# An attention stage in which scores are issued three query tiles ahead and exponentials two, over three buffers of probabilities

## The chip, the cores and the metric

One NeuronCore of a Trainium2 chip runs the whole program. The metric is the device time of one execution, in microseconds (us). TensorE (PE) does matmuls and transposes, VectorE (DVE) maxima, divisions and subtractions, ScalarE (ACT) exponentials and copies, GpSimd (POOL) some copies and subtractions; SyncE (SP) issues the DMAs.

## The reference

One layer of a streaming encoder over 1024 tokens with 1024 features: a norm and an input projection, four retention heads, four attention heads, an output projection, a feed-forward part, a gated embedding and a last norm. The change touches only the attention heads:

```python
def attend(args):
    q_blk, b = args                                   # 128 queries
    q_chunk = (b * Q_BLOCK + jnp.arange(Q_BLOCK)) // CHUNK
    mask = key_chunk[None, :] <= q_chunk[:, None]     # causal by chunks of 64
    s = jnp.einsum('bqhd,bkhd->bhqk', q_blk, k).astype(jnp.float32) * scale
    s = jnp.where(mask[None, None], s, neg)
    prob = jax.nn.softmax(s, axis=-1).astype(v.dtype)
    return jnp.einsum('bhqk,bkhe->bqhe', prob, v)
```

Query tile t (0 to 7) sees the first (t+1)*128 keys, so tile 0 has 128 columns of scores and tile 7 has 1024. All is float32: a projection or a score is taken as hi*hi + hi*lo + lo*hi, with each operand split by ACT (the high part, a cast) and DVE (the rest, a subtraction).

## The kernel before, in words

Five engines run five instruction streams written out by hand, which meet at counting semaphores. Each stream is in order. The attention stage has four heads; heads 0 to 2 are iterations of a loop and head 3 stands by itself after it. One head is one pass of `pe_head` (line 1016), `act_head` (1077) and `dve_head` (1115), each with its own loop over the eight query tiles:

- `scores(t)` on PE (line 1032): five matmuls into one bank of PSUM for tiles 0 to 3, ten into two banks for tiles 4 to 7. `SCORE_BANK` (line 1009) names the first bank. From tile 4 on, banks are used again, and the matmuls wait for an earlier exponential (`a_exp`).
- `biggest(t)` on DVE (lines 1122 to 1127): masks the corner, takes the row maximum and scales it into a bias.
- `exp(t)` on ACT (line 1083): the exponential into a buffer of probabilities, t % 2 of two, and the row's sum; `divide(t)` on DVE (lines 1139 and 1142) divides by it in place.
- `turn(t)` on PE (line 1039): t+1 transposes of the probabilities into banks 4 and 5; ACT copies them out (line 1111), which raises `a_pt`.
- `values(t)` on PE (line 1048): 2(t+1) short matmuls, which wait for that copy. `out_hi(t)` on ACT (line 1088) and `out_lo(t)` on DVE (line 1133) split the result.

The order of PE in heads 0 to 2, before: scores 0, 1, 2; scores 3, turn 0; values 0, turn 1; scores 4, values 1, turn 2; scores 5, values 2, turn 3; scores 6, values 3, turn 4; scores 7, values 4, turn 5; next head's queries, first half, values 5, turn 6; second half of the queries, values 6, turn 7; both halves of the next head's keys, values 7. A half of the queries is six matmuls of 512 columns and a half of the keys three, all at line 860.

The order of ACT, before: exp 0; then for each t: exp t+1, out_hi t-1, the work of that step, and the copy of turn t. The work of a step is `early` at t = 3 (the casts of the next head's projection weights, lines 951 and 952), `out_weights_hi` at t = 4 and 5 (line 1070), and `late` at t = 7, which is the two casts of the next head's queries (line 983, `head_hi(e, h + 1, 0)`); `late` stands ahead of the copy of turn 7. After the loop come the casts of the keys and of the rotary rows, and out_hi 7.

The order of DVE, before: biggest 0, biggest 1, divide 0; then for each t: biggest t+2, divide t+1, out_lo t-1, and `early` at t = 3 (lines 956 and 958, the rest of the two weights).

In head 3 the two halves of the queries are replaced by transposes of the retention output (line 1235, four to a tile of 128 tokens): tiles 0 and 1 ahead of values 5, tiles 2 and 3 ahead of values 6; ACT and DVE take them out with `turned(0)` and `turned(1)`. After turn 7 comes the output projection (lines 206 to 208).

Of the kernel before, what the change touches and what calls it, by code (L numbers as in the profile page):

```python
# [17 lines left out]
ACT = mybir.ActivationFunctionType  # L18
AXX = mybir.AxisListType.X

P = 128
S = 1024
D = 1024
T = S // P
# [50 lines left out]
def build(nc, t_in, out):  # L75
    ctx = ExitStack()
    with ctx:
# [35 lines left out]
        def tmp(a, n):  # L113
            return TMP[:, a:a + n]
# [891 lines left out]

            return (1, (t + 1) * P) if t < 4 else (2, (t + 1) * P // 2)

        SCORE_BANK = (2, 0, 3, 1, 2, 0, 2, 0)

        def score_banks(t):

# [3 lines left out]
        def pe_head(e, h, early, after):  # L1016
            def scores(t):
                if t in (0, 3):
                    e.wait_ge(a_lo, h * 4 + (4 if t else 3))
                if t in (0, 2):  # L1020
                    e.wait_ge(a_qr, h * 2 + (2 if t else 1))
                if t >= 4:
                    e.wait_ge(a_exp, h * T + t - 1)
                tok = slice(t * P, t * P + P)
                nb, n = seen(t)
                for c in range(nb):

                    blk = slice(c * n, c * n + max(n, 2 * P))
                    dst = bank(SCORE_BANK[t] + c, max(n, 2 * P))
                    for i, (a, b) in enumerate(((QT[0], KT[0]), (QT[0], KT[1]), (QT[1], KT[0]),  # L1030
                                                (QR, CT[0][:, 3]), (QR, CT[1][:, 3]))):
                        last = nc.tensor.matmul(dst, a[:, tok], b[:, blk], start=(i == 0), stop=(i == 4))  # L1032
                last.then_inc(a_scores, 1)

            def turn(t):
                e.wait_ge(a_prob, h * T + t + 1)
                e.wait_ge(a_pt, h * T + t)
                for j in range(t + 1):
                    last = nc.tensor.transpose(PS[:, 4 + j // 4, (j % 4) * P:(j % 4) * P + P],  # L1039
                                               tmp((t % 2) * 1024 + j * P, P), ident)  # L1040
                last.then_inc(a_turn, 1)

            def values(t):
                e.wait_ge(a_vh, h * 2 + (1 if t < 2 else 2))
                e.wait_ge(a_pt, h * T + t + 1)
                e.wait_ge(a_o_lo, h * T + max(0, t - 1))
                for j in range(t + 1):
                    last = nc.tensor.matmul(bank(6 + t % 2, P), VH[:, j], PT[t % 2][:, j * P:j * P + P], start=(j == 0), stop=(j == t))  # L1048
                last.then_inc(a_pv, 1)

            for t in range(3):
                scores(t)
            for t in range(T):
                if t == 0:
                    scores(3)
                elif 2 <= t < T - 2:
                    scores(t + 2)
                elif t >= T - 2:

                    e.wait_ge(a_exp, h * T + T - 1)  # L1060
                    early(t + 2 - T)
                if t >= 1:
                    values(t - 1)
                turn(t)
            e.wait_ge(a_exp, h * T + T)
            after(lambda: values(T - 1))
# [10 lines left out]
        def act_head(e, h, early, late, after, turned=None):  # L1077
            def exp(t):
                e.wait_ge(a_bias, h * T + t + 1)
                e.wait_ge(a_turn, h * T + max(0, t - 1))  # L1080
                nb, n = seen(t)
                dst = tmp((t % 2) * 1024, nb * n).rearrange("p (b n) -> p b n", b=nb)
                nc.scalar.activation(dst, score_banks(t), ACT.Exp, bias=ST[:, 76 + t % 2:77 + t % 2],
                                     scale=SCALE, accum_out=ST[:, 78 + t % 2:79 + t % 2]).then_inc(a_exp, 1)

            def out_hi(t):
                e.wait_ge(a_pv, h * T + t + 1)
                nc.scalar.copy(HTH[:, bass.ds(h + 4, 1), t * P:t * P + P],
                               bank(6 + t % 2, P).unsqueeze(1)).then_inc(a_o_hi, 1)

            exp(0)
            for t in range(T):
                if t + 1 < T:
                    exp(t + 1)
                if turned and t == T - 1:
                    turned(1)
                if t >= 1:
                    out_hi(t - 1)
                if turned and t == T - 2:
                    turned(0)  # L1100
                if t == 3:
                    early()
                if t in (4, 5):
                    out_weights_hi(e, h, t - 4)
                if t == T - 1:
                    late()
                e.wait_ge(a_turn, h * T + t + 1)
                e.wait_ge(a_pv, h * T + max(0, t - 1))
                n = (t + 1) * P
                src = PS[:, 4:6, :].rearrange("p b n -> p (b n)")[:, 0:n]  # L1110
                nc.scalar.copy(PT[t % 2][:, 0:n], src).then_inc(a_pt, 1)
            after()
            out_hi(T - 1)

        def dve_head(e, h, early, after, turned=None):
            def biggest(t):
                e.wait_ge(a_scores, h * T + t + 1)
                e.wait_ge(a_exp, h * T + max(0, t - 1))
                src = score_banks(t)
                nb, n = seen(t)  # L1120

                nc.vector.memset(src[0:CHUNK, nb - 1, n - CHUNK:n], MASKED).then_inc(a_mask, 1)
                e.wait_ge(a_mask, h * T + t + 1)
                nc.vector.tensor_reduce(ST[:, 74 + t % 2:75 + t % 2], src, mybir.AxisListType.XY if nb > 1 else AXX,
                                        ALU.max).then_inc(a_max, 1)
                e.wait_ge(a_max, h * T + t + 1)
                nc.vector.tensor_scalar(ST[:, 76 + t % 2:77 + t % 2], ST[:, 74 + t % 2:75 + t % 2], -SCALE, None,
                                        ALU.mult).then_inc(a_bias, 1)

            def out_lo(t):  # L1130
                e.wait_ge(a_o_hi, h * T + t + 1)
                d = slice(t * P, t * P + P)
                nc.vector.tensor_tensor(HTL[:, bass.ds(h + 4, 1), d], bank(6 + t % 2, P).unsqueeze(1),
                                        HTH[:, bass.ds(h + 4, 1), d].bitcast(F32), ALU.subtract).then_inc(a_o_lo, 1)

            def divide(t):
                e.wait_ge(a_exp, h * T + t + 1)
                n = (t + 1) * P
                nc.vector.reciprocal(ST[:, 80 + t % 2:81 + t % 2], ST[:, 78 + t % 2:79 + t % 2]).then_inc(a_rec, 1)
                e.wait_ge(a_rec, h * T + t + 1)  # L1140
                p = tmp((t % 2) * 1024, n)
                nc.vector.tensor_scalar(p, p, ST[:, 80 + t % 2:81 + t % 2], None, ALU.mult).then_inc(a_prob, 1)

            biggest(0)
            biggest(1)
            divide(0)
            for t in range(T):
                if t + 2 < T:
                    biggest(t + 2)
                if t + 1 < T:  # L1150
                    divide(t + 1)
                if turned and t == T - 1:
                    turned(1)
                if t >= 1:
                    out_lo(t - 1)
                if turned and t == T - 2:
                    turned(0)
                if t == 3:
                    early()
            after()  # L1160
            out_lo(T - 1)

        def pe_3b(e):
            e.wait_ge(b_v_out, T)
            head_keys(e, 0, [0])
            rotary_turn(e, T - 1)
            e.wait_ge(b_qr, 5)
            head_keys(e, 0, [1])

            def next_keys(values, h):  # L1170
                head_keys(e, h)
                values()
            with e.Fori(0, HEADS - 1) as h:
                pe_head(e, h, lambda b: head_queries(e, h + 1, b), lambda values: next_keys(values, h + 1))
            e.wait_ge(r_done, NR)

            def first_turns(b):
                if b:
                    e.wait_ge(a_exp, NR)
                pe_retention_turn(e, (2 * b, 2 * b + 1))  # L1180

            def out_products(values):
                out_product(e, 0)
                values()
                pe_retention_turn(e, (4, 5))
                out_product(e, 1)
                pe_retention_turn(e, (6, 7))
            pe_head(e, HEADS - 1, first_turns, out_products)
# [1366 lines left out]
```

## Time and profile before

| | us |
|---|---|
| median of 3 runs | 1249.16 (1249.0 to 1249.78) |
| profiled execution, its own time | 1250.04 |
| profiled execution, span of the instructions | 1248.2 |
| PE busy by the page | 1235.0 (99%) |
| PE weight loads busy | 1042.3 (84%) |
| attention stage, from the first scores to the output projection | about 283 to 393 |

A row of the timeline gives the start, the length, the engine, the line, what is written and read, and how many instructions were merged; in square brackets stands the idle time before it and what ended it. A matmul's length includes its way through the array, so consecutive matmuls overlap in the rows, and the time that PE gives to one is read from the distance between starts. The windows view gives the busy time of each engine in a stretch.

### The profile page before, as it was taken

How to read it: one execution, taken by the hardware profiler on the slowest of the kernel's cores; microseconds unless marked ns; L12 is line 12 of the kernel's file. 1: busy time of each engine (PE TensorE's matmuls, PEld its weight loads, DVE VectorE, ACT ScalarE, POOL GpSimd, SP SyncE). 2: the span in 40 equal slices, each digit the busy share in tenths (PEclk: the TensorE clock that was granted, in tenths of full speed). 3: DMA queues.
4: the chain of work that ended last, by engine and by line, in shares of the span. 5: the costliest groups of instructions: out<-in, count | busy, mean ns of one | idle time of the engine just before them, and what ended most of it. 6: DMA issues, size and time to landing. Idle time of an engine off the chain costs nothing.

```text
span 1248.2 us, 16786 instructions
## 1 busy us (share of the span) xinstructions
PE 1235.0 (99%) x6014; PEld 1042.3 (84%) x6014; DVE 721.0 (58%) x1176; ACT 483.3 (39%) x892; POOL 516.2 (41%) x519
## 2 busy tenths in 40 slices
PE   9999999999999999999999999999999999999997
PEld 8888888888888888888888888888888888888886
DVE  5544444466664437855544455444489999954433
ACT  6622222256564224533333333333354344424422
POOL 3533443351110003555533455433499889810011
PEclk9999999999999999999999999999999999999999
DMA  9511101000021500242332342422554545420002
GB/s 342 166 34 42 44 2 43 1 10 26 17 92 62 152 1 1 76 127 93 118 114 70 113 127 85 127 85 85 185 192 160 171 169 187 150 85 1 1 34 101
DMA packets 101931, 115.09 MB, mean 92 GB/s; under 512 B 4832, under 2 KB 67680, under 8 KB 101856
## 3 DMA queue, kind: packets, MB, share of 16 engines
q1 hardware_dynamic: 101424, 113.57, 27.8%
q8 instruction: 45, 0.74, 0.2%
q10 hardware_dynamic: 432, 0.54, 0.1%
q14 instruction: 30, 0.25, 0.1%
HBM read 90.49 MB, written 23.59 MB: 91 GB/s over the span
## 4 chain that ended last, share of the span: by engine, by line
PE 95%; DVE 2%; ACT 1%; POOL 1%; issue 1%; DMA 0%; POOLq 0%; SPq 0%; DVEq 0%; ACTq 0%
PE PS L1738 11%; PE PS L1739 11%; PE PS L1737 11%; PE PS L208 8%; PE PS L206 8%; PE PS L207 8%; PE PS L2071 5%; PE PS L2073 5%; PE PS L2072 5%; PE PS L1032 3%; PE PS L1048 3%; PE PS L2450 2%; PE PS L2448 2%; PE PS L2449 2%; PE PS L2463 2%; PE PS L1039 1%
## 5 line engine op out<-in xcount | busy, mean ns | idle before, releaser
L206 PE MATMUL PS<-WF,HTH 128*128 128x512 f32 (+1 forms) x448 | 176.9, 395 | 0.5 <-DVE HTL L436 0.3
L208 PE MATMUL PS<-WF,HTL 128*128 128x512 f32 (+1 forms) x448 | 173.7, 388 | 0.0
L207 PE MATMUL PS<-WF,HTH 128*128 128x512 f32 (+1 forms) x448 | 173.3, 387 | 0.0
L1458 DVE TENSOR_TENSOR X<-X,PS 128x512 f32<-128x512 f32 x172 | 110.3, 679 | 53.4 <-PE PS L208 35.4
L1738 PE MATMUL PS<-HTL,WF 128*128 128x512 f32 x336 | 130.9, 389 | 0.0
L1737 PE MATMUL PS<-HTH,WF 128*128 128x512 f32 x336 | 130.9, 389 | 0.0
L1739 PE MATMUL PS<-HTH,WF 128*128 128x512 f32 x336 | 130.8, 389 | 0.0
L1670 DVE TENSOR_TENSOR WF<-RAW,WF 128x512 fp32r<-128x512 f32 x63 | 70.8, 1125 | 77.5 <-ACT WF L1660 77.5
L1739 PE MATMUL PS<-WF 128*128 128x512 f32 x252 | 98.1, 389 | 0.0
L1738 PE MATMUL PS<-WF 128*128 128x512 f32 x252 | 98.1, 389 | 0.0
L1737 PE MATMUL PS<-WF 128*128 128x512 f32 x252 | 98.1, 389 | 0.0
L206 PEld LDWEIGHTS PS<-WF,HTH 128*128 128x128 f32 x448 | 84.3, 188 | 16.4 <-DVE HTL L436 0.6
L208 PEld LDWEIGHTS PS<-WF,HTL 128*128 128x128 f32 x448 | 84.1, 188 | 16.3
L207 PEld LDWEIGHTS PS<-WF,HTH 128*128 128x128 f32 x448 | 84.3, 188 | 15.0
L1878 POOL TENSOR_TENSOR TMP<-TMP 128x512 f32<-128x512 f32 x10 | 16.1, 1608 | 160.3 <-DVE TMP L1862 160.3
L2072 PE MATMUL PS<-HTL,HTH 128*128 128x512 f32 x200 | 77.9, 389 | 0.0
L2071 PE MATMUL PS<-HTH 128*128 128x512 f32 x200 | 77.9, 389 | 0.0
L2073 PE MATMUL PS<-HTH,HTL 128*128 128x512 f32 x200 | 77.9, 389 | 0.0
L707 ACT ACTIVATE TMP<-PS,ST 128x384 f32<-128x384 f32 x32 | 18.6, 580 | 152.0 <-PE PS L208 152.0
L1737 PEld LDWEIGHTS PS<-HTH,WF 128*128 128x128 f32 x336 | 63.1, 188 | 13.1
L1738 PEld LDWEIGHTS PS<-HTL,WF 128*128 128x128 f32 x336 | 63.1, 188 | 13.1
L1739 PEld LDWEIGHTS PS<-HTH,WF 128*128 128x128 f32 x336 | 63.1, 188 | 13.0
(266 smaller groups left out, 2814.4 us busy)
## 6 DMA issues: line engine op xcount, KB each, us to landing
hid<-TMP SPq DMA_DIRECT2D x74, 256.0 KB, 2.3
TMP<-hid SPq DMA_DIRECT2D x25, 512.0 KB, 4.5
RAW<-in_w_ffn_gate SPq DMA_DIRECT2D x22, 512.0 KB, 4.0
RAW<-in_w_ffn_up SPq DMA_DIRECT2D x22, 512.0 KB, 5.3
RAW<-in_w_ffn_down SPq DMA_DIRECT2D x22, 512.0 KB, 4.1
X<-in_x SPq DMA_DIRECT2D x16, 512.0 KB, 6.6
RAW<-in_w_in SPq DMA_DIRECT2D x32, 256.0 KB, 3.8
TAB<-hid SPq DMA_DIRECT2D x9, 512.0 KB, 4.5
```

What stands on the lines that cost most here:

```text
L206: nc.tensor.matmul(dst, HTH[:, k, tok], w_h, start=(k == 0), stop=False)
L207: nc.tensor.matmul(dst, HTH[:, k, tok], w_l, start=False, stop=False)
L208: last = nc.tensor.matmul(dst, HTL[:, k, tok], w_h, start=False, stop=(k == K - 1))
L1032: last = nc.tensor.matmul(dst, a[:, tok], b[:, blk], start=(i == 0), stop=(i == 4))
L1458: nc.vector.tensor_tensor(x, x, src, ALU.add).then_inc(done, 1)
L1670: nc.vector.tensor_tensor(part(name, 1), part_raw(j, name), part(name, 0).bitcast(F32), ALU.subtract).then_inc(f_w_lo, 1)
L1737: nc.tensor.matmul(dst, w_h, m_h, start=(first and k == 0), stop=False, skip_group_check=True)
L1738: nc.tensor.matmul(dst, w_h, m_l, start=False, stop=False, skip_group_check=True)
L1739: last = nc.tensor.matmul(dst, w_l, m_h, start=False, stop=(k == 3), skip_group_check=True)
L2071: nc.tensor.matmul(dst, h_h, w_h, start=(q < 3 and k == 0), stop=False, skip_group_check=True)
L2072: nc.tensor.matmul(dst, h_h, w_l, start=False, stop=False, skip_group_check=True)
L2073: last = nc.tensor.matmul(dst, h_l, w_h, start=False, stop=(k == 1), skip_group_check=True)
```

## The change

- PE issues `scores(t + 3)` at step t, for t up to 4. Scores 4 move ahead of values 0, scores 5 ahead of values 1, and so on; each waits for the exponential that frees its banks (scores 4 for exp 1, scores 5 for exp 3, scores 6 for exp 4, scores 7 for exp 5).
- Tile 1 scores go to bank 3 and tile 2 scores to bank 0.
- The next head's queries go to steps 5 and 6, and the first half of its keys to step 7, ahead of values 6; the second half stays ahead of values 7. In head 3 retention tiles 0 and 1 go to step 5, tile 2 to step 6, tile 3 to step 7.
- ACT does exp 0 and exp 1 first and then exp t+2 at step t. `early` goes from step 3 to step 2 on ACT and on DVE. `late` stays at step 7.
- Probabilities, biases and sums have three buffers, t % 3; the third buffer of probabilities is the space `JUNK` (the tables of the angles, no longer in use). DVE's maximum and ACT's exponential wait one tile less.

```diff
-        SCORE_BANK = (2, 0, 3, 1, 2, 0, 2, 0)
+        SCORE_BANK = (2, 3, 0, 1, 2, 0, 2, 0)
+        BIAS, SUMS = 85, 88
+        def probs(t):
+            return JUNK if t % 3 == 2 else tmp((t % 3) * 1024, 1024)
 ...
                 if t >= 4:
-                    e.wait_ge(a_exp, h * T + t - 1)
+                    e.wait_ge(a_exp, h * T + (2 if t == 4 else t - 1))
 ...
             for t in range(T):
-                if t == 0:
-                    scores(3)
-                elif 2 <= t < T - 2:
-                    scores(t + 2)
-                elif t >= T - 2:
-                    e.wait_ge(a_exp, h * T + T - 1)
-                    early(t + 2 - T)
+                if t < T - 3:
+                    scores(t + 3)
+                else:
+                    e.wait_ge(a_exp, h * T + (T if t == T - 1 else T - 1))
+                    early(t + 3 - T)
                 if t >= 1:
                     values(t - 1)
                 turn(t)
 ...
             def exp(t):
                 e.wait_ge(a_bias, h * T + t + 1)
-                e.wait_ge(a_turn, h * T + max(0, t - 1))
+                e.wait_ge(a_turn, h * T + max(0, t - 2))
 ...
             exp(0)
+            exp(1)
             for t in range(T):
-                if t + 1 < T:
-                    exp(t + 1)
+                if t + 2 < T:
+                    exp(t + 2)
 ...
-                if t == 3:
+                if t == 2:
                     early()
 ...
             def biggest(t):
                 e.wait_ge(a_scores, h * T + t + 1)
-                e.wait_ge(a_exp, h * T + max(0, t - 1))
+                e.wait_ge(a_exp, h * T + max(0, t - 2))
 ...
+            def next_queries(b, h):
+                if b < 2:
+                    head_queries(e, h, b)
+                else:
+                    head_keys(e, h, [0])
             def next_keys(values, h):
-                head_keys(e, h)
+                head_keys(e, h, [1])
                 values()
 ...
             def first_turns(b):
                 if b:
                     e.wait_ge(a_exp, NR)
-                pe_retention_turn(e, (2 * b, 2 * b + 1))
+                pe_retention_turn(e, (b + 1,) if b else (0, 1))
```

## Rows read from the trace of the kernel before

**Rows 1.** The page: busy time of each engine, share of the span, instructions.
```profile
PE 1235.0 (99%) x6014; PEld 1042.3 (84%) x6014; DVE 721.0 (58%) x1176; ACT 483.3 (39%) x892; POOL 516.2 (41%) x519
```
**Rows 2.** Windows: head 1 and head 3; length, busy per engine, PEclk, DMA.
```profile
311.43:339.87 28.44, 27.76 (x190) 25.29 (x188) 18.40 (x55) 17.65 (x43) 3.54 (x3) 1.00 0.06 18
368.26:392.61 24.35, 23.68 (x171) 22.00 (x170) 16.67 (x51) 14.44 (x36) 3.61 (x3) 1.00 0.34 122
```
**Rows 3.** Timeline of the start of head 1: start, length, engine, line.
```profile
314.72 0.19 ACT L1083 ACTIVATION_READ_ACCUMULATOR TMP<-PS,ST 128x1 f32 x1
314.76 0.33 PE L1039 MATMUL PS<-CST,TMP 128*128 128x128 f32 x1
...
315.13 0.27 ACT L1111 COPY TMP<-PS 128x128 f32<-128x128 f32 x1 [0.22 <-PE PS L1039]
...
315.50 0.46 PE L1048 MATMUL PS<-TMP,GB 128*128 128x128 f32 x2 [0.40 <-issue]
...
316.12 0.44 PE L1039 MATMUL PS<-CST,TMP 128*128 128x128 f32 x2 [0.16 <-DVE TMP L1142]
...
316.36 0.71 PE L1032 MATMUL PS<-HTL 128*128 128x320 f32 x3
...
317.13 0.69 ACT L1083 ACTIVATE TMP<-PS,ST 128x512 f32<-128x512 f32 x1 [0.16 <-DVE ST L1127]
```
**Rows 4.** Timeline of head 1, steps 2 to 5.
```profile
317.94 0.61 PE L1048 MATMUL PS<-TMP,GB 128*128 128x128 f32 x4
...
318.33 0.82 DVE L1124 TENSOR_REDUCE ST<-PS 128x1 f32<-128x640 f32 x1
...
318.62 0.77 PE L1032 MATMUL PS<-HTL 128*128 128x384 f32 x3
...
319.37 0.80 ACT L1083 ACTIVATE TMP<-PS,ST 128x640 f32<-128x640 f32 x1
...
319.85 0.28 DVE L1133 TENSOR_TENSOR HTL<-PS,HTH 128x128 f32 x1
...
321.42 0.27 ACT L1088 CAST HTH<-PS 128x128 f32 x1 [1.16 <-PE PS L1048]
321.49 0.85 PE L1032 MATMUL PS<-HTL 128*128 128x448 f32 x3
321.62 0.41 ACT L951 CAST WF<-RAW 128x256 fp32r x1
...
322.14 0.58 ACT L1111 COPY TMP<-PS 128x512 f32<-128x512 f32 x1
...
322.78 0.41 DVE L956 TENSOR_TENSOR WF<-RAW,WF 128x256 fp32r<-128x256 f32 x1
...
324.96 0.93 PE L1032 MATMUL PS<-HTL 128*128 128x512 f32 x3
```
**Rows 5.** Timeline of the end of head 1.
```profile
332.51 1.63 PE L860 MATMUL PS<-WF 128*128 128x512 f32 x6
...
332.80 0.91 ACT L1111 COPY TMP<-PS 128x896 f32<-128x896 f32 x1 [0.41 <-PE PS L1039]
...
336.34 1.64 PE L860 MATMUL PS<-WF 128*128 128x512 f32 x6
...
336.95 1.05 ACT L1111 COPY TMP<-PS 128x1024 f32<-128x1024 f32 x1
...
338.09 2.02 PE L1048 MATMUL PS<-TMP,GB 128*128 128x128 f32 x16
```
**Rows 6.** Timeline of the end of head 3.
```profile
385.52 1.04 PE L1235 MATMUL PS<-CST,X 128*128 128x128 f32 x8
...
386.44 1.13 ACT L1083 ACTIVATE TMP<-PS,ST 128x1024 f32<-128x1024 f32 x1
...
386.66 1.58 PE L1048 MATMUL PS<-TMP,GB 128*128 128x128 f32 x12
...
390.04 1.80 PE L1048 MATMUL PS<-TMP,GB 128*128 128x128 f32 x14 [0.17 <-issue]
```

More of the change, by code:

```diff
@@ L1039, in turn @@
                     last = nc.tensor.transpose(PS[:, 4 + j // 4, (j % 4) * P:(j % 4) * P + P],
-                                               tmp((t % 2) * 1024 + j * P, P), ident)
+                                               probs(t)[:, j * P:j * P + P], ident)
                 last.then_inc(a_turn, 1)
@@ L1079, in exp @@
                 e.wait_ge(a_bias, h * T + t + 1)
-                e.wait_ge(a_turn, h * T + max(0, t - 1))
+                e.wait_ge(a_turn, h * T + max(0, t - 2))
                 nb, n = seen(t)
-                dst = tmp((t % 2) * 1024, nb * n).rearrange("p (b n) -> p b n", b=nb)
-                nc.scalar.activation(dst, score_banks(t), ACT.Exp, bias=ST[:, 76 + t % 2:77 + t % 2],
-                                     scale=SCALE, accum_out=ST[:, 78 + t % 2:79 + t % 2]).then_inc(a_exp, 1)
+                dst = probs(t)[:, 0:nb * n].rearrange("p (b n) -> p b n", b=nb)
+                nc.scalar.activation(dst, score_banks(t), ACT.Exp, bias=ST[:, BIAS + t % 3:BIAS + 1 + t % 3],
+                                     scale=SCALE, accum_out=ST[:, SUMS + t % 3:SUMS + 1 + t % 3]).then_inc(a_exp, 1)
             def out_hi(t):
@@ L1126, in biggest @@
                 e.wait_ge(a_max, h * T + t + 1)
-                nc.vector.tensor_scalar(ST[:, 76 + t % 2:77 + t % 2], ST[:, 74 + t % 2:75 + t % 2], -SCALE, None,
+                nc.vector.tensor_scalar(ST[:, BIAS + t % 3:BIAS + 1 + t % 3], ST[:, 74 + t % 2:75 + t % 2], -SCALE, None,
                                         ALU.mult).then_inc(a_bias, 1)
@@ L1138, in divide @@
                 n = (t + 1) * P
-                nc.vector.reciprocal(ST[:, 80 + t % 2:81 + t % 2], ST[:, 78 + t % 2:79 + t % 2]).then_inc(a_rec, 1)
+                nc.vector.reciprocal(ST[:, 80 + t % 2:81 + t % 2], ST[:, SUMS + t % 3:SUMS + 1 + t % 3]).then_inc(a_rec, 1)
                 e.wait_ge(a_rec, h * T + t + 1)
-                p = tmp((t % 2) * 1024, n)
+                p = probs(t)[:, 0:n]
                 nc.vector.tensor_scalar(p, p, ST[:, 80 + t % 2:81 + t % 2], None, ALU.mult).then_inc(a_prob, 1)
@@ L1157, in dve_head @@
                     turned(0)
-                if t == 3:
+                if t == 2:
                     early()
@@ L1168, in pe_3b @@
             head_keys(e, 0, [1])
+            def next_queries(b, h):
[3 more added lines that the diff above has]
+                    head_keys(e, h, [0])
             def next_keys(values, h):
-                head_keys(e, h)
+                head_keys(e, h, [1])
                 values()
             with e.Fori(0, HEADS - 1) as h:
-                pe_head(e, h, lambda b: head_queries(e, h + 1, b), lambda values: next_keys(values, h + 1))
+                pe_head(e, h, lambda b: next_queries(b, h + 1), lambda values: next_keys(values, h + 1))
             e.wait_ge(r_done, NR)
```

## The prediction, made before the changed kernel was built

> **What bounds the kernel now.** I read the page first: PE is busy for 1235.0 of 1248.2 us [rows 1], so whatever lengthens or shortens PE's stream changes the time one for one, and no change of order can win more than PE's idle time. The change adds and removes no matmul. Then the windows: head 1 takes 28.44 us from its first scores to those of head 2, with DVE busy for 18.40 and ACT for 17.65; head 3 takes 24.35 us up to the output projection [rows 2]. PE shows 27.76 of 28.44 us, an idle time of 0.68. That understates it, since the length of a matmul in a row includes its way through the array. I therefore took stalls from starts. A matmul of 512 columns takes 0.23 us of PE (0.09 more once per group), and a short one (values, transposes) about 0.10: seven of them lie between 317.94 and 318.62 [rows 4]. By starts head 1 waits in three places. The transpose of tile 0 starts at 314.76 and values 0 only at 315.50; two short matmuls later turn 1 starts at 316.12 [rows 3]. That is 0.62 and 0.33 us of waiting. And values 7 starts at 338.09, although six projections begun at 336.34 need 1.47 [rows 5]: 0.28 us.
>
> The Trainium skill (Trainium Kernel Development and Optimization, section Performance Expectations) says that matmul busy time is a bad measure because matmuls are pipelined, and that weight loads' busy time is a good one. Head 1 shows 25.29 us of them, 3.15 below the length [rows 2]. Taken as room that would be three times what I count by starts; most of it lies beside matmuls of 512 columns, so I keep the starts.
>
> All times below are us after the start of a head; head 1 starts at 311.43 [rows 2].
>
> **Part 1, the start of a head: what is removed comes back.** Scores 4 (1.58 us, 316.36 to 317.94) now stand between turn 0, at 3.33, and values 0. They wait for exp 1, whose last instruction ends at 314.91, 3.48 in [rows 3]: start 3.53, a wait of 0.1, end 5.11. ACT now does exp 2 ahead of copy 0 (old: 315.13), so that copy ends near 5.05 (an estimate: exp 2 lies half way between exp 1 and exp 3), just in time. Values 0 and turn 1 end at 5.55, and the old waits of 0.95 are gone. But scores 5 now stand next, and they wait for exp 3. Its row says what released it: a bias from DVE, at 5.70 [rows 3]. DVE's list up to there (three maxima, two divisions) is in the same order as before, so exp 3 does not come earlier. It ends at 6.39, its sum 0.09 later (as in the accumulator's row), and scores 5 start at 6.53: a wait of 0.98. In the old order scores 5 started at 318.62, 7.19 in, with values 1 and turn 2 (0.68) already done [rows 4]. The new one has these still ahead: 6.53 + 0.68 = 7.21. Nothing is gained. Bounds: -0.95 if DVE's bias came a microsecond earlier, which no row suggests, and 0; I take 0.
>
> **Part 2, scores 7 wait for exp 5: +0.85 in heads 0 to 2.** From exp 3 on, ACT and DVE release each other in a ring: exp t+2, out_hi t-1, out_lo t-1, the next maximum. After exp 3 (6.48) come out_hi 0 (0.27, of which 0.1 overlaps) and out_lo 0 (0.28 and about 0.15 to start): the maximum of tile 4 starts at 7.10. From the mask to the exponential it takes 0.15 + 1.04 (318.33 to 319.37), then exp 4 takes 0.80 + 0.09: end 9.19. The casts of the next head's weights, `early`, now come here, with out_hi 1 (0.20 to the next start) and 0.6 for both (321.62 to 322.14 and a tail) to 9.95; DVE's two subtractions (0.41 and a shorter one) last to 10.65 [rows 4]. Only then comes the maximum of tile 5, which stands behind them on DVE. With 0.13 us more for each further 128 columns in maximum and exponential, exp 5 runs from 12.0 to 13.0, and scores 7 can start at 13.05. PE is there earlier: scores 5 take 1.85 (321.49 - 318.62, less ten short matmuls), values 1 and turn 2 0.68, to 9.06; scores 6 wait for exp 4 until 9.24 and take 2.12 (324.96 - 321.49, less thirteen short ones); with values 2 and turn 3 that is 12.38. The wait is 0.7. The old scores 7 started at 13.53 with values 3 and turn 4 (1.35) done [rows 4]; the new state is 14.40, 0.87 later. Bounds: 0.1, if the ring takes 0.7 less, and 1.2, if each of its five hand-overs costs 0.07 more than read; I take 0.85.
>
> **Part 3, exp 7 goes ahead of copy 5: +0.2 in heads 0 to 2.** The maximum of tile 7 stands behind out_lo 3, which waits for values 3. By the same ring exp 7 ends near 20.2, 0.4 after ACT could have begun out_hi 4, and copy 5 is late by about 0.2 for values 5. Bounds 0 and 0.5.
>
> **Part 4, half as much work covers the copies at the end: +0.5 and +0.7 in heads 0 to 2.** The copy of tile 6 starts 0.29 after the six projections behind turn 6 and takes 0.91 (332.51, 332.80), so values 6 can start 1.30 after these [rows 5]. Six matmuls cover 1.47; now three keys matmuls stand there, 3 x 0.23 + 0.09 = 0.78: a wait of 0.52. Behind turn 7 ACT does the two casts of the queries before the copy, because `late` stays where it is, so values 7 start 1.75 after the projections (336.34 to 338.09) whatever PE does in between. They covered 1.47 and now cover 0.78: a wait of 0.97 in place of 0.28. The Trainium skill (TensorE: Matmul & The Clock Gate, Architectural detail) says that ACT and DVE are strict first-in, first-out queues. If ACT took the copy ahead of the casts, values 7 would wait some 0.5 less; the rows agree with the page, since the copy begins at 336.95, 0.6 after turn 7 had made way. Bounds of both waits together: 1.0 and 1.4. The moved queries save nothing: at their old places nothing waited.
>
> **Part 5, head 3: +1.8.** Nothing is cast at step 2, so scores 7 need not wait. At the end the cover is thinner. In the old order eight transposes (385.52 to 386.40) leave values 5 a wait of 0.26, a second eight leave values 6 0.33, and exp 7 runs at 386.44, after copy 5 [rows 6]. In the new one values 4 stand behind eight transposes (a wait of 0.3), values 5 behind four (0.45 us) and behind ACT's exp 7 (1.13), out_hi 4, a weight cast and copy 5 (a wait of 1.2 in all), values 6 behind four and one retention cast (0.8). That is 2.3 less 0.6: 1.7, with 0.1 of part 1's small waits. Bounds 0.6 and 2.6.
>
> **Sum.** Heads 0 to 2: 0.85 + 0.2 + 0.5 + 0.7 = 2.25 and 0.05 of small waits, 2.3 each, 6.9; head 3 1.8; together +8.7. The buffers cost no instruction, and SP's w_o loads wait for POOL as before, off the path. The profiled execution took 1250.04 and its span 1248.2, which would give a span of 1256.9; from the median of 1249.16 I predict 1257.9. The low ends give 3 x 1.1 + 0.6 = +3.9 (1253.1), the high ends 3 x 3.1 + 2.6 = +11.9 (1261.1).
>
> **Rivals.** A: the ring is faster than read and scores 7 do not wait, while the covers at the end still fall short: 8.7 - 3 x 1.05 = +5.5, 1254.7. For it: DVE has 10 of 28 us free. Against it: these are waits in a ring, not work. B: the waits at the head's start really go (-0.95 x 3 - 0.6 = -3.4), because the bias of tile 3 comes before PE is done with values 0, and only the ends cost (+3.6, and little in head 3): 1249.4. It decides at exp 3: it would have to end by 5.5 in place of 6.48. C, the other side: PE's run ahead absorbs everything, copies included, and all stalls go: 3 x 1.23 + 1.15 in head 3 = -4.8, less for head 0, so 1244.7. It decides at the copy of tile 7: it would have to be done 0.7 us earlier than the casts ahead of it allow. For it speaks only that a third buffer loosens two waits of ACT; no row shows ACT or DVE waiting for a buffer. D: DVE's or ACT's ring falls behind further than the bounds, each step costing PE up to 0.5 more: 1263. E: the change does nothing, because each stall only moves: 1249.2.
>
> **Chances.** The forecast 0.66, A 0.14, B and E together 0.10, C 0.07, D 0.03. The range runs from 1252.5 to 1261.5, with A inside and B to E (2 in 10) outside. About 0.2% (2.5 us) is what a measurement of this kernel can tell from no change: faster 0.07, same 0.10, slower 0.83.
>
> **What would show it.** Right: scores 5 start within 0.1 us of exp 3's accumulator read, 6.5 after the head's start; scores 7 start right behind exp 5; values 6 and values 7 start 1.3 and 1.75 after the keys' first matmul, the three matmuls of which end well before; a head of 30.7 us in place of 28.44 and PE's total busy time nearly unchanged. Wrong: scores 7 issued without a wait (A), or exp 3 earlier than 5.7 (B).

## The result: 10 us slower, and where the profile of the changed kernel shows it

| | before | changed |
|---|---|---|
| median, us | 1249.10 (6 runs, 1248.98 to 1249.78) | 1259.15 (6 runs, 1258.73 to 1259.38) |
| span of the profiled execution | 1248.2 | 1257.2 |
| its own time | 1250.04 | 1259.04 |

The ratio is 1.0079, with a 95% interval of 1.0069 to 1.0089. The forecast was 1257.9.

The page of the changed kernel, busy time of each engine (against rows 1), and the windows of head 1 and head 3 (against rows 2):

```profile
PE 1236.8 (98%) x6014; PEld 1040.1 (83%) x6014; DVE 721.0 (57%) x1176; ACT 482.5 (38%) x892; POOL 516.4 (41%) x519
```
```profile
313.30:344.28 30.98, 28.67 (x189) 25.09 (x188) 18.54 (x55) 17.38 (x43) 3.88 (x3) 1.00 0.06 17
375.24:401.61 26.37, 24.04 (x171) 21.99 (x170) 16.75 (x51) 14.37 (x36) 3.76 (x3) 1.00 0.32 112
```

Head 1 takes 30.98 us in place of 28.44, head 3 26.37 in place of 24.35 [rows 2]; heads 0 and 2 are longer by 2.54 and 2.57. Together the four heads take 9.67 us more. From the start of the output projection to the end both profiles take 855.59 us (1257.2 - 401.61 and 1248.2 - 392.61), so nothing is lost or won behind the stage. In front of it the changed kernel's profile is 0.67 us shorter (the first scores start at 282.59 and not 283.26), although no instruction there differs. That is a difference between executions, and with it the spans differ by 9.0.

The same engines do the same work in more time: DVE's and ACT's busy times hardly move. PE's own busy time even rises in head 1, from 27.76 to 28.67, though PE now waits more. A matmul's length includes its way through the array, and where the next one comes late, that way no longer lies under it. The weight loads keep their time in head 1 (25.29 us before, 25.09 now), so their share falls from 89% to 81%. The Trainium skill (Trainium Kernel Development and Optimization, Performance Expectations) says that weight loads' busy share and not matmul busy time tells how far a kernel is from full speed. These rows agree: matmul busy time rose while PE did the same work, and what the weight loads leave free of the head rose from 3.15 to 5.89 us, by 2.74 for a head that is 2.54 longer. Where PE waits is read from the starts.

The three largest waits of PE in the stage (who waited for whom, us in total, times, longest):

```profile
PE PS L1053 <- issue: 4.8, 8, 0.8
PE PS L1037 <- ACT TMP L1085: 2.8, 4, 0.7
PE PS L1037 <- ACT TAB L1085: 1.3, 3, 0.4
```

L1053 are the values, L1037 the scores, L1085 is the exponential. Scores now wait for exponentials; the same view of the kernel before has no such wait, only 1.8 us of values waiting and 0.3 of turns. "issue" ahead of values stands for ACT's copy: in the rows below the copy ends 0.1 us before each such start. The head's start, in the timeline of head 1 (start, length; the head begins at 313.30):

```profile
316.83 0.71 PE L1037 MATMUL PS<-HTL 128*128 128x320 f32 x3
...
318.07 0.26 ACT L1114 COPY TMP<-PS 128x128 f32<-128x128 f32 x1
...
318.43 0.46 PE L1053 MATMUL PS<-TMP,GB 128*128 128x128 f32 x2
318.72 0.38 PE L1044 MATMUL PS<-CST,TMP 128*128 128x128 f32 x2
...
318.99 0.69 ACT L1085 ACTIVATE TMP<-PS,ST 128x512 f32<-128x512 f32 x1 [0.67 <-DVE ST L1130]
...
319.58 0.19 ACT L1085 ACTIVATION_READ_ACCUMULATOR TMP<-PS,ST 128x1 f32 x1
...
319.82 0.79 PE L1037 MATMUL PS<-HTL 128*128 128x384 f32 x3 [0.72 <-ACT TMP L1085]
```

The reader is to see that the waits of rows 3 are gone (scores 4 at 316.83, values 0 and turn 1 right behind) and that one of the same size stands in their place. Turn 1 begins at 318.72 and takes 0.22, so PE is free at 318.94. Exp 3 begins 5.69 us into the head as before (5.70), its sum is read out by 319.77, and scores 5 start at 319.82, after 0.88 us of waiting. Steps 2 to 4:

```profile
321.58 0.79 ACT L1085 ACTIVATE TMP<-PS,ST 128x640 f32<-128x640 f32 x1 [1.39 <-DVE ST L1130]
...
322.59 0.41 ACT L951 CAST WF<-RAW 128x256 fp32r x1
...
323.35 0.42 DVE L956 TENSOR_TENSOR WF<-RAW,WF 128x256 fp32r<-128x256 f32 x1 [0.25 <-ACT WF L952]
...
323.98 0.11 DVE L1125 MEMSET PS<- 64x64 f32 x1
...
325.31 0.90 ACT L1085 ACTIVATE TAB<-PS,ST 128x768 f32<-128x768 f32 x1 [1.73 <-DVE ST L1130]
...
326.11 0.19 ACT L1085 ACTIVATION_READ_ACCUMULATOR TAB<-PS,ST 128x1 f32 x1
...
326.35 0.96 PE L1037 MATMUL PS<-HTL 128*128 128x512 f32 x3 [0.40 <-ACT TAB L1085]
```

This is the ring: casts on ACT, then their subtractions on DVE, only then the mask and maximum of tile 5 (from 323.98), exp 5, and scores 7 at 326.35. And the head's end:

```profile
337.03 0.94 PE L860 MATMUL PS<-WF 128*128 128x512 f32 x3
...
337.31 0.91 ACT L1114 COPY TMP<-PS 128x896 f32<-128x896 f32 x1 [0.41 <-PE PS L1044]
338.32 1.80 PE L1053 MATMUL PS<-TMP,GB 128*128 128x128 f32 x14 [0.34 <-issue]
...
340.75 0.94 PE L860 MATMUL PS<-WF 128*128 128x512 f32 x3
...
341.36 1.05 ACT L1114 COPY TMP<-PS 128x1024 f32<-128x1024 f32 x1
...
342.50 2.02 PE L1053 MATMUL PS<-TMP,GB 128*128 128x128 f32 x16 [0.81 <-issue]
```

Three keys matmuls begin at 337.03 and values 6 start 1.29 later; three begin at 340.75 and values 7 start 1.75 later, the same distance as from 336.34 to 338.09 before [rows 5], with half as much work in it.

### The profile page after: what moved, and what is told of

Same layout as the page of the kernel before. It is cut to its first block, busy times and chain, and to the rows that moved or that the text cites. A ratio compares the mean times of both kernels' runs of the same rounds, so it can differ in the third digit from the quotient of the medians.

```text
span 1257.2 us, 16787 instructions
## 1 busy us (share of the span) xinstructions
PE 1236.8 (98%) x6014; PEld 1040.1 (83%) x6014; DVE 721.0 (57%) x1176; ACT 482.5 (38%) x892; POOL 516.4 (41%) x519
## 4 chain that ended last, share of the span: by engine, by line
PE 92%; DVE 3%; issue 2%; ACT 2%; POOL 1%; DMA 0%; DVEq 0%; ACTq 0%; POOLq 0%; SPq 0%
PE PS L1747 11%; PE PS L1746 11%; PE PS L1748 11%; PE PS L206 8%; PE PS L208 8%; PE PS L207 8%; PE PS L2082 5%; PE PS L2080 5%; PE PS L2081 5%; PE PS L1053 2%; PE PS L2459 2%; PE PS L2458 2%; PE PS L2457 2%; PE PS L2472 2%; PE PS L1037 2%
```

## The experiments

Two questions were open: whether each term of the sum has the cause that the prediction gave it, and whether anything of the idea could be kept. In the labels a_ is an edit of the changed kernel and b_ one of the kernel before; the runs of before beside them had medians of 1249.18 to 1249.58.

**a_early3** undoes the move of the weights' casts.

```diff
-                if t == 2:
+                if t == 3:
                     early()
 ...
-                if t == 2:
+                if t == 3:
                     early()
```

The first place is ACT's, the second DVE's.

> The changed kernel (1259.15 us) with the casts of the next head's weights (early) back at step 3 on ACT and DVE. Theory (ring): the casts stand in the ring between exp 4 and the maximum of tile 5, so without them exp 5 ends about 1 us earlier and scores 7 no longer wait (0.56 us by starts in each of heads 0 to 2): -1.7, with up to 0.3 given back at exp 6: 1257.6. Rival (the wait for exp 5 has its cause in the order of exponentials and copies on ACT, not in the casts): unchanged, 1259.2.

Measured: 1257.93 us (ratio to before 1.0072, 1.0058 to 1.0086), 1.2 less than the changed kernel by the medians, though the slowest run (1258.94) reaches into the range of the changed kernel. In the profile each of heads 0 to 2 is 0.28 to 0.31 shorter and head 3 as long as in the changed kernel. The timeline of head 1:

```profile
323.93 0.91 ACT L1085 ACTIVATE TAB<-PS,ST 128x768 f32<-128x768 f32 x1 [1.32 <-DVE ST L1130]
...
325.19 0.94 PE L1037 MATMUL PS<-HTL 128*128 128x512 f32 x3
...
329.41 1.65 PE L860 MATMUL PS<-WF 128*128 128x512 f32 x6 [0.22 <-ACT TMP L1085]
```

Exp 5 begins 11.14 us into the head in place of 12.01, and scores 7 start without a wait, as the theory wanted, so the casts were what made scores 7 wait. Part of the gain comes back one step later: the casts now delay exp 6, and the queries wait for it, 0.38 us by starts. Moving the casts moves the wait and makes it smaller.

**a_keysback** puts the first half of the keys back behind turn 7.

```diff
                     head_queries(e, h, b)
-                else:
-                    head_keys(e, h, [0])
 ...
-                head_keys(e, h, [1])
+                head_keys(e, h)
                 values()
```

> The changed kernel with the first half of the next head's keys back behind turn 7, in heads 0 to 2. Theory (the cover is only divided anew): values 6 then wait 1.30 in place of 0.52 and values 7 0.28 in place of 0.98, together +0.1 per head: 1259.4. Rival (it is the early keys that cost, and values 6 would not wait without them): both waits go back to those of the kernel before, -1.2 per head, 1255.5.

Measured: 1259.46 us (1.0081, 1.0067 to 1.0095), no different from the changed kernel. In the timeline values 6 and values 7 of head 1:

```profile
339.00 1.80 PE L1053 MATMUL PS<-TMP,GB 128*128 128x128 f32 x14 [1.19 <-ACT TMP L1114]
...
343.18 2.02 PE L1053 MATMUL PS<-TMP,GB 128*128 128x128 f32 x16
```

Values 6 wait 1.35 and values 7 0.29, against 0.51 and 0.98 in the changed kernel: 1.64 in place of 1.49. The early keys are not what costs. What fits both divisions is that the run-ahead makes one more gap to cover. Before, all scores were issued by step 5 and eighteen projection matmuls covered three copies (5, 6 and 7). Now the scores are all issued by step 4 and the same eighteen must cover four.

**a_latefirst** puts ACT's casts of the next head's queries ahead of out_hi 6.

```diff
+                if t == T - 1:
+                    late()
                 if t >= 1:
                     out_hi(t - 1)
 ...
-                if t == T - 1:
-                    late()
                 e.wait_ge(a_turn, h * T + t + 1)
```

> The changed kernel with ACT's casts of the next head's queries (late) ahead of out_hi 6 in place of behind it. Theory (ACT's order): the copy of tile 7 then starts 0.3 after turn 7 and not 0.6, values 7 start 1.44 and not 1.75 after the keys' matmuls begin, and their wait falls from 0.98 to 0.66: -0.3 per head, 1258.2. Rival (the copy is held up by something else, as its own length or a buffer): 1259.2.

Measured: 1258.13 us (1.0071, 1.0057 to 1.0085), 1.0 less than the changed kernel, and its slowest run (1258.48) is below that kernel's fastest (1258.73). The rows of head 1:

```profile
340.24 0.94 PE L860 MATMUL PS<-WF 128*128 128x512 f32 x3
...
340.52 1.01 ACT L1114 COPY TMP<-PS 128x1024 f32<-128x1024 f32 x1 [0.52 <-PE PS L1044]
...
341.63 2.02 PE L1053 MATMUL PS<-TMP,GB 128*128 128x128 f32 x16 [0.46 <-issue]
```

The copy now begins 0.28 after the keys' first matmul and is released by PE's turn, where it began 0.61 after it, straight from the casts. Values 7 follow at 1.39 in place of 1.75, 0.36 earlier; the prediction had put this order at some 0.5. The statement quoted in the prediction from the Trainium skill (TensorE: Matmul & The Clock Gate, Architectural detail), that ACT takes its instructions strictly in order, is borne out: changing that order alone moved the copy.

**a_narrowmax** shortens DVE's list in front of exp 3; it leaves out part of the maxima.

```diff
+                if t < 4:
+                    src = src[:, :, 0:P]
                 nc.vector.tensor_reduce(ST[:, 74 + t % 2:75 + t % 2], src, mybir.AxisListType.XY if nb > 1 else AXX,
 ...
```

The lines left out put the factor 0.05 on the scale of tiles 0 to 3, in the exponential and in the bias.

> The changed kernel with the row maxima of tiles 1 to 3 taken over the first 128 columns alone (and a softmax scale a twentieth of the right one for tiles 0 to 3, so that nothing overflows): it leaves out part of the maximum. By the lengths of the reductions exp 3 comes 0.13 + 0.27 + 0.40 = 0.8 us earlier. Theory (scores 5 wait for exp 3, which DVE's list sets): the wait of 0.88 falls to 0.1 in all four heads and everything behind moves with it: -3.1, 1256.0. Rival (PE would be held there by a copy or the bank all the same): 1259.2.

Measured: 1255.94 us (1.0053, 1.0039 to 1.0067), 3.2 less. In head 1:

```profile
317.49 0.69 ACT L1085 ACTIVATE TMP<-PS,ST 128x512 f32<-128x512 f32 x1 [0.26 <-DVE ST L1132]
...
318.32 0.79 PE L1037 MATMUL PS<-HTL 128*128 128x384 f32 x3 [0.16 <-ACT TMP L1085]
```

Exp 3 is still released by DVE, and scores 5 again start 0.14 after its end, but the wait fell from 0.88 to 0.32 in heads 1 and 2 and is gone in heads 0 and 3 (head 0 waits 0.21 before scores 6 instead). In head 1 scores 5 start 0.80 earlier in the head than in the changed kernel (5.72 and not 6.52). The wait shrank by 0.56 of that; the rest is that PE reaches the place sooner, since scores 4 too wait for an exponential whose maximum is now shorter. The waits before scores 7 and at the head's end stayed as they were.

**b_narrowmax** does the same to the kernel before.

> The kernel before with the same narrow maxima of tiles 1 to 3 (and the same twentieth of the softmax scale for tiles 0 to 3); it leaves out part of the maximum. Theory (in the old order the start of a head waits first for copy 0, which DVE's maxima of tiles 1 to 3 do not set, and for 0.33 us for the division of tile 1): only that second wait goes, in heads 1 and 2, and 0.07 in the others: -0.8, 1248.3. Rival (DVE's list sets the start of a head whatever PE's order): -3, 1246.

Measured: 1248.30 us (0.9992, 0.9983 to 1.0001), 0.9 less by the medians, though the interval includes no change. The wait of 0.62 before values 0 is still there in each head (0.56 here) and the wait of 0.33 before turn 1 is gone. So the same shortening is worth 3.2 us in the changed order and less than 1 in the old one: only in the changed order is PE held by DVE's list at that place.

**b_actahead** keeps of the change ACT's and DVE's part alone; PE's order is that of before (a diff against the changed kernel). The lines left out put back the banks, the wait of scores 4, both halves of the keys behind turn 7 and the retention tiles two and two.

```diff
 ...
-                if t < T - 3:
-                    scores(t + 3)
-                else:
-                    e.wait_ge(a_exp, h * T + (T if t == T - 1 else T - 1))
-                    early(t + 3 - T)
+                if t == 0:
+                    scores(3)
+                elif 2 <= t < T - 2:
+                    scores(t + 2)
+                elif t >= T - 2:
+                    e.wait_ge(a_exp, h * T + T - 1)
+                    early(t + 2 - T)
 ...
```

> The changed kernel with PE's order of before (scores two ahead, queries at steps 6 and 7, both key halves behind turn 7, retention tiles two and two, banks of before), so only the exponentials two ahead, the three buffers and the early weights are left of the change. Theory (an exponential two ahead stands in front of the copy that values wait for, and needs its scores a step earlier to be free): each copy waits for the maximum and the exponential of the scores just made, 0.8 us more before values 0 and about 1, 0.4, 0.7 and 1.6 before values 2 to 5: +4.5 per head, 1267. Rival (ACT's order is free as long as it has idle time, and the cost of the change is PE's order alone): 1249.

Measured: 1261.78 us (1.0100, 1.0084 to 1.0115). The start of head 1, ACT and PE:

```profile
318.05 0.58 ACT L1088 ACTIVATE TAB<-PS,ST 128x384 f32<-128x384 f32 x1 [0.72 <-DVE ST L1133]
...
318.62 0.26 ACT L1117 COPY TMP<-PS 128x128 f32<-128x128 f32 x1
```
```profile
317.17 0.33 PE L1044 MATMUL PS<-CST,TMP 128*128 128x128 f32 x1
318.97 0.46 PE L1053 MATMUL PS<-TMP,GB 128*128 128x128 f32 x2 [1.47 <-issue]
```

Copy 0 stands behind exp 2, which waits for DVE, and values 0 wait 1.69 us, 1.07 more than before; that was expected. By starts the waits before values 2 to 5 are 0.92, 0.15, 0.2 and 1.07, where 1, 0.4, 0.7 and 1.6 were expected. The mechanism holds: the copy that values 2 wait for, at 323.82, stands behind exp 4, which waited 1.65 for DVE, and behind the casts of `early` (0.5 us). The total came out at +12.6 and not +18, because the sizes of the later waits were too high. A likely reason, not tested, is that each wait delays PE and so leaves the next copy more time.

**a_actold** is the other half: PE's scores three ahead, ACT's exponentials one ahead as before.

```diff
             exp(0)
-            exp(1)
             for t in range(T):
-                if t + 2 < T:
-                    exp(t + 2)
+                if t + 1 < T:
+                    exp(t + 1)
```

> The changed kernel with ACT's exponentials one tile ahead as before (exp t+1 at step t), all else as changed, so PE's scores run three ahead alone. Theory (the waits form a ring through banks: scores t+3 wait for exp t+1, which now stands behind the copy of tile t-1, which waits for PE's turn t-1): every step from scores 6 on waits for a whole round trip, by the same reckoning 1.7 us before scores 6, 1.9 before scores 7, 2.5 before the next head's queries: about +8 per head against 1249, 1280. Rival (the exponentials' lead is what costs, PE's alone is free): 1249 to 1253.

Measured: 1289.51 us (1.0326, 1.0311 to 1.0342). By starts head 1 waits 1.35 before scores 5, 1.98 before scores 6, 1.73 before scores 7 and 2.30 before the queries, and the head's end keeps its 0.51 and 0.98. The expectation had named 1.7, 1.9 and 2.5 and left out the first and the last two, and it had not foreseen a fall of PE's clock (last section). Each half of the change alone is worse than both together (1261.78 and 1289.51 against 1259.15). The banks bind the two leads to each other: from scores 5 on, scores t+3 need exp t+1 out of their way. No run has the third buffer by itself, so what it does alone is not shown.

**a_turns22** divides head 3's retention tiles two and two.

```diff
-                if b:
+                if b == 1:
                     e.wait_ge(a_exp, NR)
-                pe_retention_turn(e, (b + 1,) if b else (0, 1))
+                if b < 2:
+                    pe_retention_turn(e, (2 * b, 2 * b + 1))
```

> The changed kernel with head 3's retention tiles two ahead of values 4, two ahead of values 5 and none ahead of values 6 (two, one, one in the changed kernel). Theory (the cover is only divided anew): values 5 wait 0.4 less and values 6 0.4 more: 1259.2. Rival (the division of the retention tiles is what makes head 3 2.0 us longer): 1258.2 or less.

Measured: 1259.40 us (1.0076, 1.0062 to 1.0090), no different from the changed kernel. In head 3 values 5 and values 6:

```profile
396.15 1.57 PE L1053 MATMUL PS<-TMP,GB 128*128 128x128 f32 x12 [0.27 <-issue]
...
399.69 1.80 PE L1053 MATMUL PS<-TMP,GB 128*128 128x128 f32 x14 [1.20 <-ACT TMP L1114]
```

By starts values 5 wait 0.47 in place of 0.86 and values 6 1.35 in place of 0.77. The wait went from the one to the other, as with the keys: the same cover divided anew.

**b_split** asks what the lead in scores can be used for. It starts from the kernel before and moves half of scores 4 up, one bank of two; ACT and DVE keep their order.

```diff
-        SCORE_BANK = (2, 0, 3, 1, 2, 0, 2, 0)
+        SCORE_BANK = (2, 3, 0, 1, 2, 0, 2, 0)
 ...
-            def scores(t):
+            def scores(t, halves=None):
 ...
-                    e.wait_ge(a_exp, h * T + t - 1)
+                    e.wait_ge(a_exp, h * T + (2 if t == 4 else t - 1))
 ...
-                for c in range(nb):
+                for c in halves or range(nb):
 ...
-                last.then_inc(a_scores, 1)
+                if halves != (0,):
+                    last.then_inc(a_scores, 1)
 ...
                     scores(3)
-                elif 2 <= t < T - 2:
+                elif t in (1, 2):
+                    scores(4, (t - 1,))
+                elif 3 <= t < T - 2:
                     scores(t + 2)
```

> The kernel before (1249.1 us) with half of scores 4 (the bank of tile 0) moved ahead of values 0 and the other half left ahead of values 1; tiles 1 and 2 change banks as in the changed kernel; ACT's and DVE's order is that of before. Theory (exp 3 is the floor of a head's start, at 6.5 us, and the old order reaches scores 5 only at 7.19): half of scores 4 (0.75) fills the wait before values 0 and the other half the wait for copy 1, and scores 5 start at 6.53 with everything else done: -0.66 per head, less in heads 0 and 3 (0.5): 1246.8. Rival (moving scores up only moves the wait, as in the changed kernel): 1249.1.

Measured: 1246.65 us (0.9979, 0.9970 to 0.9988), 2.5 less than before. Head 1 begins at 310.13:

```profile
313.66 0.71 PE L1032 MATMUL PS<-HTL 128*128 128x320 f32 x3
...
314.50 0.38 PE L1049 MATMUL PS<-TMP,GB 128*128 128x128 f32 x2
...
314.81 0.44 PE L1040 MATMUL PS<-CST,TMP 128*128 128x128 f32 x2
...
315.00 0.68 PE L1032 MATMUL PS<-HTL 128*128 128x320 f32 x3
...
315.82 0.62 PE L1049 MATMUL PS<-TMP,GB 128*128 128x128 f32 x4
...
316.67 0.77 PE L1032 MATMUL PS<-HTL 128*128 128x384 f32 x3
```

Every group follows the one before it: half of scores 4, values 0, turn 1, the other half, values 1, turn 2, scores 5 at 6.54 in the head in place of 7.19. They start 0.08 after the sum of exp 3 is read out (316.59), so PE meets this floor with a wait of 0.1 at most. Both waits at the head's start are filled and nothing is taken from the head's end; in the profile the four heads are 0.66, 0.68, 0.62 and 0.61 shorter than in the kernel before.

**b_split_ends** adds the order of ACT at the end, as an edit of b_split.

```diff
+                if t == T - 1:
+                    late()
                 if t >= 1:
                     out_hi(t - 1)
-                if turned and t == T - 2:
-                    turned(0)
 ...
-                if t in (4, 5):
-                    out_weights_hi(e, h, t - 4)
-                if t == T - 1:
-                    late()
 ...
                 nc.scalar.copy(PT[t % 2][:, 0:n], src).then_inc(a_pt, 1)
+                if turned and t == T - 2:
+                    turned(0)
+                if t in (4, 5):
+                    out_weights_hi(e, h, t - 4)
```

> As b_split, and on ACT three copies of turned probabilities go ahead of casts that nobody waits for: the query casts stand ahead of out_hi 6 (as in a_latefirst), the output weights' casts behind copies 4 and 5, and in head 3 the cast of retention tile 0 behind copy 6. Theory (values wait for copies that stand behind casts): values 7 lose their wait of 0.28 in heads 0 to 2, and head 3 its waits of 0.26 and 0.33: -1.4 against b_split, 1245.4. Rival (these casts come back as waits of DVE, POOL or exponentials): equal to b_split.

Measured: 1245.65 us (0.9972, 0.9961 to 0.9983), the fastest of all and 3.5 under the kernel before. The step from b_split is 1.0, less than their intervals are wide, but the two sets of times do not overlap (1245.46 to 1246.26, and 1246.46 to 1246.84). The wait of values 7 is gone in heads 0 to 2, which is 0.85 by starts. Head 3 kept its two waits (0.23 and 0.33), against the expectation:

```profile
381.53 1.04 PE L1238 MATMUL PS<-CST,X 128*128 128x128 f32 x8
...
381.73 0.80 ACT L1110 COPY TMP<-PS 128x768 f32<-128x768 f32 x1 [0.39 <-PE PS L1040]
...
382.63 1.58 PE L1049 MATMUL PS<-TMP,GB 128*128 128x128 f32 x12
```

ACT is idle for 0.39 before this copy and is released by PE's turn, so no cast held it. The copy's own way from turn to values (1.1 us) is longer than eight transposes.

## Why the prediction was right

The measured 1259.15 lies between 1252.5 and 1261.5, and the mechanism came out as told in every part that a run took apart; only small terms were mis-sized. The predicted figure stands in brackets behind the measured one.

- **Part 1** held to 0.01 us in head 1: exp 3 at 5.69 (5.70), scores 5 at 6.52 (6.53), no gain at the start. a_narrowmax and b_narrowmax show the cause. PE reached the place at 5.64 (5.55), so the wait was 0.88 (0.98).
- **Part 2**: scores 6 at 9.22 (9.24), exp 5 from 12.01 to 13.00 (12.0 to 13.0), scores 7 at 13.05 (13.05). a_early3 shows that without the casts at this step scores 7 do not wait. PE was ready later than reckoned and waited 0.56 (0.7), with the four transposes ahead of it counted at the 0.11 us that lie between their starts; the place in time is as predicted, and the loss against before is 0.91 at the start of the queries (0.87).
- **Part 3**: values 5 wait 0.19 in heads 0 to 2 (0.2). The timeline of the changed kernel's head 1 has the ring: out_hi 3 at 329.94, released by values 3, out_lo 3 at 330.36, the mask of tile 7 at 330.66, exp 7 from 332.25 to 333.45 (20.15 into the head, 20.2), out_hi 4 right behind it, copy 5 at 334.02. But a weight cast of 0.5 us (333.50) stands between out_hi 4 and the copy too, and no run took the two apart, so how much of the 0.19 is exp 7's stays open.
- **Part 4**: 0.51 and 0.98 (0.52 and 0.97), with 1.29 and 1.75 from the keys' first matmul (1.30 and 1.75). a_keysback shows that it is the cover and not the place of the keys, a_latefirst that the second wait hangs on ACT's order.
- **Part 5**: head 3 is 2.02 longer (1.8), and a_turns22 shows that the division of the tiles is not the cause. Its waits by starts: 0.26 before values 4 (0.3), 0.43 before the third retention tile and 0.86 before values 5 (1.2 for both), 0.77 before values 6 (0.8). Exp 7 does stand ahead of copy 5, as these rows of the changed kernel's head 3 show:

```profile
392.98 1.12 ACT L1085 ACTIVATE TMP<-PS,ST 128x1024 f32<-128x1024 f32 x1 [1.02 <-DVE ST L1130]
...
394.75 0.81 ACT L1114 COPY TMP<-PS 128x768 f32<-128x768 f32 x1
...
395.66 1.58 PE L1053 MATMUL PS<-TMP,GB 128*128 128x128 f32 x12 [0.70 <-issue]
```

- **The sum** was short by 1.0: +8.7 of heads against +9.67, and +10.05 between the medians. The mis-sized term is the small waits, put at 0.05 in each of heads 0 to 2 and 0.1 in head 3: heads 0 to 2 came out 2.54 to 2.57 longer and not 2.3. Two things were left out. Behind values 5 and values 6 the next group starts 0.08 and 0.09 later than it did where there was no wait (338.32 to turn 7 at 339.96 is 1.64, and 1.55 in the kernel before), and 0.07 of that lies between the first and the second matmul (0.18 apart in place of 0.11). And six keys matmuls in two groups take 2 x 0.78 where one group took 1.47, by the prediction's own figures 0.09 more. Between the medians and the heads another 0.4 stays open; it is within what single executions of either kernel differ by (0.8 and 0.65).
- **The rivals**: A fails, scores 7 wait. B fails at its own point, exp 3 does not end by 5.5. C fails at the copy of tile 7. E would have needed the waits only to move; the first two did just that, but the head's end added new ones. D would have needed 1263.
- **A reading of the prediction** is too large: the 3.15 us by which the weight loads fall short of head 1 are 2.6 times its waits of 1.23 by starts, not three times. Nothing in the sum rests on it.

## What to carry to other kernels

Issuing work further ahead fills a wait only if what it needs is already done, and it leaves a gap where it came from: count, before the edit, how much independent work stands behind each hand-over at the end of the loop, since the same work spread over one gap more lets every copy show. Find the floor of a stage (here the third engine's list up to exp 3, 6.5 us into the head) and move just so much work that the bottleneck engine reaches that floor with everything else done: half of one tile's scores gave 2.5 us, and the whole change, with all scores from tile 4 on one step up, lost 10. On an engine that takes its work in order, put what the bottleneck waits for ahead of what nobody waits for, and check in the rows that such a cast is really what stands in front (b_split_ends, head 3).

## What the hardware showed that was not expected

In a_actold PE's granted clock fell to half three times, in heads 0, 1 and 3, each time for a part of a head. Head 1, scores 6 and what follows (448 columns, then values), and a window inside it (PEclk, 0.50, stands ahead of the last two numbers):

```profile
332.71 0.95 PE L1037 MATMUL PS<-HTL 128*128 128x448 f32 x3 [1.81 <-ACT TMP L1085]
333.46 0.95 PE L1037 MATMUL PS<-WF 128*128 128x448 f32 x2
334.21 1.32 PE L1037 MATMUL PS<-HTL 128*128 128x448 f32 x3
335.33 0.95 PE L1037 MATMUL PS<-WF 128*128 128x448 f32 x2
336.07 1.17 PE L1053 MATMUL PS<-TMP,GB 128*128 128x128 f32 x6
```
```profile
334.00:336.00 2.00, 2.00 (x7) 1.79 (x6) 0.22 (x1) 0.00 (x0) 0.00 (x0) 0.50 0.00 0
```

From 333.46 to 336.07 seven matmuls take 0.37 us each (2.61 / 7), where the same ones take 0.21 at a granted clock of 1.00, the level of 2.4 GHz (322.52 to 324.68 in the changed kernel, ten in 2.16, with one group start); a granted clock of 0.50 is the level of 1.2 GHz. PE had waited 1.35 and 1.98 us in the seven us before. Head 2, with the same waits, kept its clock: it takes 36.50 us at a mean granted clock of 1.00, and head 1 38.10 at 0.96. So the fall in head 1 cost 1.6 us, and the same stalls can cost more or less from head to head. What decides it stays open. In the changed kernel, with waits of up to 0.98, the granted clock stayed at 1.00 in the windows of all four heads.
